# One core, a decoder block and a block of retrieved experts: activations taken two at a time and begun earlier, gathered rows placed anew, first products of a norm in another order

## The chip, the cores and the metric

One Trainium2 chip, one of its cores. The metric is the device time of one execution in microseconds (us), median of three.

## What is computed

Two transformer blocks in a row on x of 256 tokens by 2048 columns, all in float32. `rmsnorm` stands four times ahead of large products: before the first block's projections, before its feed-forward product, before the second block's projections, and before the retrieved experts.

```python
x = x + rmsnorm(mix_out, post_mix_gain)
h = rmsnorm(x, pre_ffn_gain)
f = conv_geglu_ffn(h, w_up, conv_w, conv_b, w_down)
x = x + rmsnorm(f, post_ffn_gain)
...
h = h + concat([a_out, b_out]) @ w_out
h = h + peer(rms_norm(h, g))
return rms_norm(h, final_norm_g)
```

`peer` takes for each token 128 of 16384 experts (rows of 2048 numbers in u and v) with a weight g each:

```python
act = gelu(einsum('td,tkd->tk', xt, u[ids])) * g
out = einsum('tk,tkd->td', act, v[ids])
```

## The kernel before

**Pieces.** All weights stream through SBUF in tiles of 1 MB (`fetch`, three buffers `raw`), each four pieces of 128x512. A float32 piece is split into two fp32r parts: ScalarE (ACT) copies it to `hiR` (`split_hi`, L278), VectorE (DVE) subtracts that from the piece into `loR` (`split_lo`, L286), two pieces per operation, each written out four pieces ahead of use (`LA = 4`), in rings of eight pieces (`NQ`). TensorE (PE) multiplies high by high, high by low and low by high. A piece's end raises the semaphore `piece`; `fetch` waits until the tile three before is wholly split.

**Orders.** There is no scheduler: each engine's program is written out, and steps are placed by the number of the piece beside which they stand.

**The experts.** The first 214 tokens (`TD`) go through dense products with all 16384 experts. They are cut into 128 blocks of 128 experts in three ranges (43, 43 and 42 blocks, `RANGES`). Each range has a **u stage** (four pieces per block, `wide`, L314 and L317; results into `S_`, gelu in place) and a **v stage** (`experts_out`, L1452 and L1455), also four pieces per block, in four passes over the output columns; a piece of its first pass needs its block's activation. In a u stage stand beside the products also the gates: 27 groups per range, three DVE operations each (`dve_gates`, L1329, L1335, L1340), products on PE, and a copy into `G_`. In every range the products with the gates are spread over the u stage by `GATE0` and `GATE_STEP`. The activation of a block is made by three operations on 128x214: DVE multiplies `S_` by `G_` (`dve_gated`, L1418), ACT rounds it to `ah` (`act_act`, L1426), DVE makes the low part `al` (`dve_act`, L1434). They begin twelve pieces before the v stage, one block per piece.

**The rows.** For the last 42 tokens (`TS`) the experts are gathered: 86 operations gather 126 half rows of u and 86 of v (`pool_rows`, L1494, indirect DMA, three buffers `ring`). DVE takes a dot product with each of u (L1515) and adds each of v to `vsum` (L1522). `PLACES` lists the pieces beside which they stand: 31 in the u stages, ten pieces apart, 142 in the v stages, 3.0 to 3.4 apart (one of the 173 places is that of the gelu between u and v).

**The norms.** Ahead of a norm's first product stands a chain: sums, a root, scaling of a quarter of the columns (L360) on DVE; transposes on PE (L371, `pe_norm_turn`); the high part (`act_norm_hi`, L377, semaphore `nhi`) on ACT; the low part (`dve_norm_lo`, L383, `nlo`) on DVE. While it runs, PE computes products that nobody reads (`pe_keep`, L398), `KEEP[i]` of them before and after the first transposes. Then come the first pieces, each quarter of the operand behind a wait for its `nlo`.

**Lambda.** The constants of a recurrence in the second block are made by two ACT operations (L1792, L1794) and 24 small DVE ones (`dve_lambda`), beside the first weights (pieces 0 to 63).

**The end.** The last gain (`gf`), a selection matrix and the residual `xr` are loaded by three DMAs when the third v stage begins (`end_const`); the first to need them stands 72 pieces later.

Of the kernel before, what the change touches and what calls it, by code (L numbers as in the profile page):

```python
# [13 lines left out]
T = 256  # L14
# [31 lines left out]
P_V = 0  # L46
# [43 lines left out]
NROW = 2 * ROWS  # L90
PLACES = [P_U[r] + 4 + 10 * k for r in (1, 2) for k in range((16, 15)[r - 1])]
PLACES += [P_VV[r] + (12, 3, 3)[r] + int((3.0, 3.2, 3.4)[r] * k) for r in range(3) for k in range((52, 51, 39)[r])]
SLOT = {p - P_U[0]: k for k, p in enumerate(sorted(PLACES))}
# [11 lines left out]

ATT = 16 * 8

# [9 lines left out]
def build(nc, A, out):  # L117
# [187 lines left out]
    def wide(e, g, q, X, dst, nt, order=BY_TWO):  # L305
# [13 lines left out]
        m.then_inc(S("piece"), 1)  # L319

    def stationary(e, g, q, X, dst):

        wait_piece(e, g)
        hi, lo = hiR[:, g % NQ, :], loR[:, g % NQ, :]
        for j in range(4):
            k = 4 * q + j
            wh, wl = hi[:, j * 128:(j + 1) * 128], lo[:, j * 128:(j + 1) * 128]
            e.matmul(dst, wh, X.h[:, k, :], start=(k == 0), stop=False)  # L328
            e.matmul(dst, wh, X.l[:, k, :], start=False, stop=False)  # L329
            m = e.matmul(dst, wl, X.h[:, k, :], start=False, stop=(k == KC - 1))  # L330
        m.then_inc(S("piece"), 1)

# [58 lines left out]

    KEEP = [(36, 10), (30, 6), (30, 6), (16, 6)]

# [34 lines left out]
    out_gain = [g1, g3]  # L428
    out_load = [("att_const", ATT), ("ffn_const", 32)]
    out_junk = [junk1, junk2]  # L430
# [875 lines left out]
    GATE0 = [DEC0 + 2 * DECP + 2 - 4 * 16, 1, 1]  # L1306
    GATE_STEP = [3.3, 5.6, 5.4]
    NG = -(-TD // TG)
# [88 lines left out]
    def act_gelu(e, r, s):  # L1397
# [5 lines left out]
        e.activation(S_[:, i, :], S_[:, i, :], ACT.Gelu_apprx_tanh).then_inc(S("s_gelu"), 1)  # L1403

    def dve_gated(e, r, p):
        i0, i1 = RANGES[r]
        i = p + 12
        if 0 <= i < i1 - i0 - 1:
            todo = [i]
        elif i == i1 - i0 + 1:  # L1410
            todo = [i1 - i0 - 1]
        else:
            return
        for i in todo:
            e.wait_ge(S("s_gelu"), i0 + i + 1)
            if i == 0:
                e.wait_ge(S("g_ev"), NG * (r + 1))
            e.tensor_tensor(G_[:, i, :], S_[:, i, :], G_[:, i, :], ALU.mult).then_inc(S("gated_s"), 1)  # L1418

    def act_act(e, r, p):  # L1420
        i = p + 9
        i0, i1 = RANGES[r]
        if not 0 <= i < i1 - i0:
            return
        e.wait_ge(S("gated_s"), i0 + i + 1)
        e.copy(ah[:, i, :], G_[:, i, :]).then_inc(S("a_hi"), 1)  # L1426

    def dve_act(e, r, p):
        i = p + 7
        i0, i1 = RANGES[r]  # L1430
        if not 0 <= i < i1 - i0:
            return
        e.wait_ge(S("a_hi"), i0 + i + 1)
        e.tensor_tensor(al[:, i, :], G_[:, i, :], ah[:, i, :].bitcast(F32), ALU.subtract).then_inc(S("a_lo"), 1)  # L1434

# [137 lines left out]
    def pool_gain(e, f):  # L1573

        cs = quarter(f)
        e.wait_ge(S("end_const"), 48)
# [14 lines left out]
    def pe_rows_sum(e):  # L1591

        e.wait_ge(S("sp_use"), 2 * NROW)
        e.wait_ge(S("end_const"), 48)
        e.wait_ge(S("v_sum"), 16 + 6)
        for f in range(4):
            m = e.matmul(bank[v_bank(2, 2) + f][:, :], sel4[0:GP, :], vsum[0:GP, quarter(f)], start=True, stop=True)
        m.then_inc(S("sp_sum"), 1)

    def dve_rows_sum(e):  # L1600
        e.wait_ge(S("sp_sum"), 1)
        e.wait_ge(S("end_const"), 48)
        e.wait_ge(S("xacc"), 4)
        for f in range(4):
            e.tensor_tensor(xr[:, 1, quarter(f)], xr[:, 1, quarter(f)], bank[v_bank(2, 2) + f][:, :],
                            ALU.add).then_inc(S("sp_x"), 1)

    def dve_y_sum(e, f):
        cs = quarter(f)
        for tb, n in ((0, 128), (1, TD - 128)):  # L1610
            e.wait_ge(S("y_tr"), 2 * f + tb + 1)
            if f == 0:
                e.wait_ge(S("end_const"), 48)
# [16 lines left out]
    def pe_program(e):  # L1630
        e.wait_ge(S("cst"), 3)
        pe_norm_first(e, 0, 0)
        for fb in range(4):
            pair = (2 * (fb % 2), 2 * (fb % 2) + 1)
            if fb >= 2:
                e.wait_ge(S("vt"), 2 * (fb - 1))
            for k in range(KC):
                if fb == 0:
                    pe_norm_next(e, 0, k)
                if fb == 0 and k % 4 == 0:  # L1640
                    e.wait_ge(S("nlo"), 2 * (k // 4) + 2)
                moving(e, P_V + 16 * fb + k, XA.h[:, k, :], XA.l[:, k, :], [bank[b][:, :] for b in pair], k == 0,
                       k == KC - 1)
# [49 lines left out]
        for fb in range(2):  # L1693
            for k in range(KC):
                if fb == 0:
                    pe_norm_next(e, 2, k)
                if fb == 0 and k % 4 == 0:
                    e.wait_ge(S("nlo"), 16 + 2 * (k // 4) + 2)
                moving(e, P_GV + 16 * fb + k, XB.h[:, k, :], XB.l[:, k, :],
                       [bank[2 * fb][:, :], bank[2 * fb + 1][:, :]], k == 0, k == KC - 1)  # L1700
# [36 lines left out]
        for r, (i0, i1) in enumerate(RANGES):  # L1737
# [15 lines left out]
            for f in range(4):  # L1753
# [9 lines left out]
                for i in range(n):  # L1763
                    if f == 0:
                        e.wait_ge(S("a_lo"), i0 + i + 1)
                    experts_out(e, r, f, i)
                    for y in range(3):
                        if r == 2 and n * f + i == Y_AT[y]:
                            pe_y_turn(e, y)
                    if r == 2 and n * f + i == ROWS_AT:  # L1770
                        pe_rows_sum(e)
        pe_end_turn(e)

    def act_program(e):
# [15 lines left out]
        act_norm_hi(e, 0, 3)  # L1790
        e.wait_ge(S("start_const"), 48)
        e.activation(lz[:, 16:32], lv[:, 72:88], ACT.Abs).then_inc(S("lam_a"), 1)  # L1792
        e.wait_ge(S("lam_a"), 1)
        e.activation(lz[:, 0:16], lz[:, 16:32], ACT.Exp, scale=-1.0).then_inc(S("lam_a"), 1)  # L1794
        for i in range(64):
# [4 lines left out]
        for s in range(128):  # L1800
            split_hi(e, P_QK + s + LA)
            if s == 0:
                act_values(e, 3)
            act_attention(e, s)
        for n in range(64):
# [114 lines left out]
    def dve_program(e):  # L1920
# [21 lines left out]
        for i in range(64):  # L1942
            if i + LA >= 10:
                split_lo(e, P_V + i + LA)
            dve_lambda(e, i)
        for s in range(128):
            split_lo(e, P_QK + s + LA)
            dve_attention(e, s)
        for n in range(64):
            if n:  # L1950
                split_lo(e, P_WO + n + LA)
            dve_attention(e, 128 + n)
            if n == 0:
                split_lo(e, P_WO + LA)
# [90 lines left out]
        dve_root(e, 6, st[:, 128:134])  # L2045
        e.wait_ge(S("end_const"), 48)
        e.wait_ge(S("y_out"), 3)
# [68 lines left out]
    def sp_program(e):  # L2116
# [9 lines left out]
        for n in range(NR, NT):  # L2126
            fetch(e, n)
            if n == NR:
# [3 lines left out]
                load(e, "att_const", g1[:, :], A["g_post_mix"].partition_broadcast(128))  # L2132
            elif n == P_WO // 4 + 7:
# [37 lines left out]
            elif n == P_VV[2] // 4 + 4:  # L2171
                e.wait_ge(S("piece"), P_VV[2])
                load(e, "end_const", gf[:, :], A["g_final"].partition_broadcast(128))
                load(e, "end_const", sel4[:, :], A["sel4"])
                load(e, "end_const", xr[:, :, :], xd.ap().rearrange("t p d -> p t d"))
            for p in range(3):
# [133 lines left out]
```

## Time and profile before

| | |
|---|---|
| median of 3 runs | 2891.64 us (2890.97 to 2892.91) |
| the profiled execution | 2892.64 us |
| its span in the trace | 2891.2 us |
| PE busy | 2856.7 us, 99% of the span |
| DVE, ACT, GpSimd busy | 2071.5, 1559.1, 511.2 us |
| granted TensorE clock | 0.999 |
| DMA, mean | 226 GB/s |

Busy time of PE counts the products that nobody reads too. What bounds the kernel is read from what stands between PE's products and from what PE does in the norms' chains.

### The profile page before, as it was taken

To read this page: it belongs to the slowest core of one execution; us is meant where nothing else is said; L and a number is where in the kernel's file an instruction comes from. 1 tells how busy PE (TensorE), PEld (TensorE's weight loads), DVE (VectorE), ACT (ScalarE), POOL (GpSimd) and SP (SyncE) were. 2 spreads that over 40 slices of the span, in tenths; PEclk is the share of its full clock that TensorE was granted. 3 is DMA by queue.
4 is the path that set the end of the run, shared out by engine and by line. 5 is a ranking of instruction groups with operands and counts; after the bars stand their busy time and mean duration, and the time that the engine had idled before them with its cause. 6 is when DMAs were issued, how large, how long until landed. Compare 5 with 4: busy or idle time off the path is not lost.

```text
span 2891.2 us, 45317 instructions
## 1 busy us (share of the span) xinstructions
PE 2856.7 (99%) x18442; PEld 2625.8 (91%) x18442; DVE 2071.5 (72%) x3151; ACT 1559.1 (54%) x2319; POOL 511.2 (18%) x348
## 2 busy tenths in 40 slices
PE   9999999999999999999999999999999999999998
PEld 8888888888888888899899999999999999999997
DVE  5565567666666445666589878888778987778986
ACT  4467755555555444477444656444556444556444
POOL 0011101111111000034111000443011343101631
PEclk9999999999999999999999999999999999999999
DMA  7544455555556555555655656898767898777994
GB/s 265 177 159 141 151 190 184 189 189 188 189 188 221 197 189 175 197 175 170 232 190 175 242 191 211 324 356 331 240 229 247 314 356 313 239 242 255 343 342 152
DMA packets 105658, 654.52 MB, mean 226 GB/s; under 512 B 12526, under 2 KB 13806, under 8 KB 37870
## 3 DMA queue, kind: packets, MB, share of 16 engines
q1 hardware_dynamic: 80684, 561.44, 55.2%
q0 software_dynamic: 24768, 90.19, 8.6%
q8 instruction: 147, 2.41, 0.3%
q14 instruction: 59, 0.48, 0.0%
HBM read 646.29 MB, written 4.19 MB: 225 GB/s over the span
## 4 chain that ended last, share of the span: by engine, by line
PE 82%; DVE 9%; DMA 4%; ACT 3%; issue 2%; SPq 0%; ACTq 0%; DVEq 0%
PE ps L314 26%; PE ps L317 13%; PE ps L1452 8%; PE ps L339 6%; PE ps L341 6%; PE ps L340 6%; PE ps L1455 4%; DMA ring<-in_u_rows_dram,idx 4%; DVE loR L286 4%; PE ps L329 3%; PE ps L328 3%; PE ps L330 3%; DVE ring L1515 2%; DVE hl L1434 1%; ACT hiR L278 1%
## 5 line engine op out<-in xcount | busy, mean ns | idle before, releaser
L286 DVE TENSOR_TENSOR loR<-raw,hiR 128x1024 fp32r<-128x1024 f32 x1017 | 1258.8, 1243 | 695.9 <-ACT hiR L278 692.7
L278 ACT CAST hiR<-raw 128x1024 fp32r<-128x1024 f32 x1026 | 1069.9, 1050 | 789.8 <-PE ps L317 255.3
L314 PE MATMUL ps<-XA,hiR 128*128 128x428 f32 (+1 forms) x3936 | 1240.4, 385 | 2.0 <-DVE loR L286 1.1
L317 PE MATMUL ps<-XA,loR 128*128 128x214 f32 (+1 forms) x3936 | 913.0, 271 | 0.0
L317 PEld LDWEIGHTS ps<-XA,loR 128*128 128x128 f32 x3936 | 748.0, 190 | 83.0
L314 PEld LDWEIGHTS ps<-XA,hiR 128*128 128x128 f32 x3936 | 674.0, 188 | 17.2 <-issue 1.1
L1452 PE MATMUL ps<-hl,hiR 128*128 128x428 f32 x2048 | 582.9, 365 | 9.0 <-DVE loR L286 8.8
L1455 PEld LDWEIGHTS ps<-hl,loR 128*128 128x128 f32 x2048 | 385.3, 188 | 16.3
L1455 PE MATMUL ps<-hl,loR 128*128 128x214 f32 x2048 | 383.6, 269 | 0.0
L1452 PEld LDWEIGHTS ps<-hl,hiR 128*128 128x128 f32 x2048 | 310.5, 192 | 13.2 <-issue 10.9
L1494 POOL DMA_INDIRECT ring<-in_u_rows_dram,idx x86 | 134.7, 1567 | 610.7 <-DVE ring L1515 543.5
L1494 POOL DMA_INDIRECT ring<-in_v_rows_dram,idx x86 | 165.6, 1925 | 362.2 <-DVE vsum L1522 342.4
L340 PE MATMUL ps<-loR,Y 128*128 128x512 f32 x344 | 133.9, 389 | 0.0
L339 PE MATMUL ps<-hiR,Y 128*128 128x512 f32 x344 | 133.9, 389 | 0.0
L341 PE MATMUL ps<-hiR,Y 128*128 128x512 f32 x344 | 133.9, 389 | 0.0
L1515 DVE SCALAR_TENSOR_TENSOR ring<-ring,hrep 126x1024 f32<-126x1024 f32 x86 | 104.8, 1219 | 33.0 <-DMA ring<-in_u_rows_dram,idx 32.9
L862 POOL TENSOR_TENSOR acc<-acc,acc 128x256 f32<-128x256 f32 x43 | 31.9, 741 | 468.9 <-DVE acc L816 468.9
L1522 DVE SCALAR_TENSOR_TENSOR vsum<-ring,gated,vsum 126x1024 f32<-126x1024 f32 x84 | 107.4, 1279 | 6.8 <-DMA ring<-in_v_rows_dram,idx 6.7
L328 PE MATMUL ps<-XB,hiR 128*128 128x256 f32 x384 | 110.1, 287 | 0.0
L329 PE MATMUL ps<-XB,hiR 128*128 128x256 f32 x384 | 108.8, 283 | 0.0
L330 PE MATMUL ps<-XB,loR 128*128 128x256 f32 x384 | 108.7, 283 | 0.0
L1366 ACT ACTIVATE G__145<-ps 128x344 f32<-128x344 f32 (+3 forms) x81 | 37.6, 464 | 127.5 <-PE ps L1356 127.5
(309 smaller groups left out, 3399.0 us busy)
## 6 DMA issues: line engine op xcount, KB each, us to landing
raw<-in_u_dram SPq DMA_DIRECT2D x128, 1024.0 KB, 5.0
raw<-in_v_dram SPq DMA_DIRECT2D x128, 1024.0 KB, 7.4
raw<-in_w_up_dram SPq DMA_DIRECT2D x86, 1024.0 KB, 4.8
raw<-in_w_down_dram SPq DMA_DIRECT2D x43, 1024.0 KB, 4.8
raw<-in_w_in_qk_dram SPq DMA_DIRECT2D x32, 1024.0 KB, 4.9
raw<-in_w_out_dram SPq DMA_DIRECT2D x32, 1024.0 KB, 5.0
raw<-in_w_in_dram SPq DMA_DIRECT2D x24, 1024.0 KB, 4.9
raw<-in_w_in_v_dram SPq DMA_DIRECT2D x16, 1024.0 KB, 4.9
```

What stands on the lines that cost most here:

```text
L278: e.copy(hiR[:, r:r + 2, :], raw[n % NR][:, q:q + 2, :]).then_inc(S("hi"), 1)
L286: e.tensor_tensor(loR[:, r:r + 2, :], raw[n % NR][:, q:q + 2, :], hiR[:, r:r + 2, :].bitcast(F32), ALU.subtract).then_inc(S("lo_pool" if p ...
L314: m = e.matmul(both, hi[:, j * 128:(j + 1) * 128], X.hl[:, :, k, 0:nt], start=(first and n == 0), stop=(last and n == 7), skip_group_check ...
L317: m = e.matmul(dst[:, 0:nt], lo[:, j * 128:(j + 1) * 128], X.h[:, k, 0:nt], start=False, stop=(last and n == 7), skip_group_check=True)
L328: e.matmul(dst, wh, X.h[:, k, :], start=(k == 0), stop=False)
L329: e.matmul(dst, wh, X.l[:, k, :], start=False, stop=False)
L339: e.matmul(dsts[tb], ah_, hi, start=first, stop=False)
L340: e.matmul(dsts[tb], ah_, lo, start=False, stop=False)
L341: m = e.matmul(dsts[tb], al_, hi, start=False, stop=last)
L1452: m = e.matmul(b[:, 0:2 * TD].rearrange("p (a t) -> p a t", a=2), hi[:, j * 128:(j + 1) * 128], hl[:, :, i, :], start=(i == 0), stop=False ...
L1455: m = e.matmul(b[:, 0:TD], lo[:, j * 128:(j + 1) * 128], hl[:, 0, i, :], start=False, stop=(i == i1 - i0 - 1), skip_group_check=True)
L1494: e.indirect_dma_start(ring[m % RN][:, :], None, A["u_rows" if m < NROW else "v_rows"], bass.IndirectOffsetOnAxis(ap=idx[:, m % NROW // 2, ...
```

## The change

- **Activations in pairs.** `dve_gated`, `act_act` and `dve_act` take two blocks each (128x428). In the first range they stand as before, two pieces per pair, from 13 before the v stage. In the second and third a pair stands every 3.8 pieces, from 48 before it; `act_act` three pieces later, `dve_act` five. `GATE_STEP` of these two ranges falls from 5.6 and 5.4 to 4.4, so that all gates are done by then.
- **Rows.** 52 places in the u stages: 20 from piece 4, 5.5 apart, and 6 from piece 120, 8 apart, in each. First v stage: 42 from piece 30, 3.3 apart. The other two: 6 from piece 3, 6 apart, then 40 and 27 from piece 40, 3.2 and 3.45 apart.
- **First products of a norm.** In the first and third, products with the high operand need only `nhi`, then come the ones with `loR`, then those with the low operand. In the second, the `loR` products of two pieces come first; in the fourth, the 16 products of two pieces that need only the high operand. `KEEP` is cut.
- **Lambda** moves: ACT's part to piece 20 of the query and key products, DVE's beside the first output projection.
- **Loads.** `end_const` in twelve parts, one behind each of twelve fetches; the attention's constants six tiles later, `g1` at tile 20.

```diff
-PLACES = [P_U[r] + 4 + 10 * k for r in (1, 2) for k in range((16, 15)[r - 1])]
...
+PLACES = [P_U[r] + 4 + int(5.5 * k) for r in (1, 2) for k in range(20)]
+PLACES += [P_U[r] + 120 + 8 * k for r in (1, 2) for k in range(6)]
...
-    KEEP = [(36, 10), (30, 6), (30, 6), (16, 6)]
+    KEEP = [(36, 6), (28, 3), (28, 3), (10, 3)]
...
-    GATE_STEP = [3.3, 5.6, 5.4]
+    GATE_STEP = [3.3, 4.4, 4.4]
...
+    def moving_first(e, g, i, q, first, xh, xl, dsts):
+
+        hi, lo = hiR[:, g % NQ, :], loR[:, g % NQ, :]
+        e.wait_ge(S("hi"), g // 2 + 1)
+        for tb in range(2):
+            e.wait_ge(S("nhi"), 8 * i + 2 * q + tb + 1)
+            e.matmul(dsts[tb], xh[:, half(tb)], hi, start=first, stop=False)
+        wait_piece(e, g)
+        for tb in range(2):
+            e.matmul(dsts[tb], xh[:, half(tb)], lo, start=False, stop=False)
+        for tb in range(2):
+            e.wait_ge(S("nlo"), 8 * i + 2 * q + tb + 1)
+            m = e.matmul(dsts[tb], xl[:, half(tb)], hi, start=False, stop=False)
...
+    def pair_at(r, p):
+
+        return [k for k in range(NPAIR[r]) if (2 * k - 13 if r == 0 else int(3.8 * k) - 48) == p]
...
             if j == 0:
+                e.wait_ge(S("nhi"), 8 + 2 * q + 2)
+                for c in range(2):
+                    wide_part(e, P_UP + n + c, q, XA, bank[c], T, "low")
                 e.wait_ge(S("nlo"), 8 + 2 * q + 2)
-            wide(e, P_UP + n, q, XA, bank[j], T)
+            if j < 2:
+                wide_part(e, P_UP + n, q, XA, bank[j], T, "high")
+            else:
+                wide(e, P_UP + n, q, XA, bank[j], T)
...
             if c == 0:
+                e.wait_ge(S("nhi"), 24 + 2 * q + 2)
+                for b in range(QQ):
+                    stationary_part(e, P_Q + n + b, q, XA, bank[b][:, 0:T], "high")
                 e.wait_ge(S("nlo"), 24 + 2 * q + 2)
-            stationary(e, P_Q + n, q, XA, bank[c][:, 0:T])
+            stationary_part(e, P_Q + n, q, XA, bank[c][:, 0:T], "low")
```

PE at the third norm, ahead of the products with `XB`; `x30` and `x6` are the unread products. Before:

```order
L398 MATMUL ps<-ident 128x128 x30
L371 MATMUL ps<-ident,tmp_113 128x128 x8
L398 MATMUL ps<-ident 128x128 x6
L339 MATMUL ps<-hiR,XB 128x512
L340 MATMUL ps<-loR,XB 128x512
L341 MATMUL ps<-hiR,XB 128x512
```

Now:

```order
L446 MATMUL ps<-ident 128x128 x28
L419 MATMUL ps<-ident,tmp_113 128x128 x8
L446 MATMUL ps<-ident 128x128 x3
L372 MATMUL ps<-hiR,XB 128x512 x2
L375 MATMUL ps<-loR,XB 128x512 x2
L378 MATMUL ps<-hiR,XB 128x512 x2
```

Five unread products are gone, and the two that read the low operand (L378) stand last.

DVE in the second range's v stage, between the subtractions for its pieces 18 and 22. Before:

```order
L286 TENSOR_TENSOR loR<-raw_50,hiR 128x1024
L1418 TENSOR_TENSOR G__145<-S__144,G__145 128x214
L1434 TENSOR_TENSOR hl<-G__145,hl 128x214
L1418 TENSOR_TENSOR G__145<-S__144,G__145 128x214
L1434 TENSOR_TENSOR hl<-G__145,hl 128x214
L1515 SCALAR_TENSOR_TENSOR ring_164,dots<-ring_164,hrep 126x1024
L286 TENSOR_TENSOR loR<-raw_51,hiR 128x1024
L1418 TENSOR_TENSOR G__145<-S__144,G__145 128x214
L1434 TENSOR_TENSOR hl<-G__145,hl 128x214
L1418 TENSOR_TENSOR G__145<-S__144,G__145 128x214
L1434 TENSOR_TENSOR hl<-G__145,hl 128x214
L286 TENSOR_TENSOR loR<-raw_51,hiR 128x1024
```

Now:

```order
L289 TENSOR_TENSOR loR<-raw_50,hiR 128x1024
L1482 TENSOR_TENSOR hl<-G__145,hl 128x428
L1563 SCALAR_TENSOR_TENSOR ring_165,dots<-ring_165,hrep 126x1024
L289 TENSOR_TENSOR loR<-raw_51,hiR 128x1024
L1470 TENSOR_TENSOR G__145<-S__144,G__145 128x428
L1482 TENSOR_TENSOR hl<-G__145,hl 128x428
L289 TENSOR_TENSOR loR<-raw_51,hiR 128x1024
```

Where eight short operations stood, three of twice the length do; the rest stands in the u stage ahead.

## Rows read from the trace of the kernel before

**Rows 1.** Waits of PE: by line, who released it; us in total, times, longest.
```profile
PE ps L1452 <- DVE loR L286: 8.8, 19, 0.8
```
**Rows 2.** Timeline, first norm: start, duration, engine, operation, count, [idle before <- releaser].
```profile
14.86 2.35 DVE L286 TENSOR_TENSOR loR<-raw,hiR 128x1024 fp32r<-128x1024 f32 x2
16.44 0.47 PE L339 MATMUL ps<-hiR,XA 128*128 128x512 f32 x1
...
29.59 1.29 DVE L383 TENSOR_TENSOR XA<-ps,XA 128x512 fp32r<-128x512 f32 x2 [2.60 <-ACT XA L377]
29.93 0.23 ACT L1792 ACTIVATE lz<-lv 128x16 f32<-128x16 f32 x1
30.18 1.28 ACT L1794 ACT_TABLE_LOAD   x1
...
31.60 3.87 ACT L278 CAST hiR<-raw 128x1024 fp32r<-128x1024 f32 x4
...
33.94 0.50 PE L339 MATMUL ps<-hiR,XA 128*128 128x512 f32 x1 [1.83 <-DVE loR L286]
```
**Rows 3.** Timeline, third norm, PE and DVE.
```profile
1151.97 1.42 DVE L360 SCALAR_TENSOR_TENSOR tmp<-x,st,g 128x512 f32<-128x512 f32 x2
1153.24 1.04 PE L371 MATMUL ps<-ident,tmp 128*128 128x128 f32 x8
...
1154.49 1.29 DVE L383 TENSOR_TENSOR XB<-ps,XB 128x512 fp32r<-128x512 f32 x2 [0.45 <-ACT XB L377]
...
1155.84 0.50 PE L339 MATMUL ps<-hiR,XB 128*128 128x512 f32 x1 [0.22 <-DVE XB L383]
```
**Rows 4.** Timeline, fourth norm, PE.
```profile
1451.69 2.65 PE L371 MATMUL ps<-ident,tmp 128*128 128x128 f32 x16
1454.17 1.50 PE L398 MATMUL ps<-ident 128*128 128x128 f32 x12
1455.43 0.36 PE L328 MATMUL ps<-XA,hiR 128*128 128x256 f32 x1
```
**Rows 5.** Stretches: us, busy PE, PEld, DVE, ACT, POOL, clock, DMA share, GB/s.
```profile
30.00:36.00 6.00, 4.17 (x19) 3.14 (x18) 4.19 (x7) 5.44 (x8) 0.00 (x0) 1.00 0.15 35
1787.00:1822.00 35.00, 35.00 (x229) 34.08 (x229) 35.00 (x73) 21.55 (x41) 6.76 (x5) 1.00 0.74 254
2047.00:2110.00 63.00, 63.00 (x527) 60.80 (x526) 47.85 (x72) 34.49 (x57) 6.63 (x5) 1.00 0.72 244
```
**Rows 6.** Timeline of DVE: a late row of the first v stage, then the third.
```profile
1992.23 1.23 DVE L1515 SCALAR_TENSOR_TENSOR ring<-ring,hrep 126x1024 f32<-126x1024 f32 x1 [2.83 <-DMA ring<-in_u_rows_dram,idx]
...
2689.49 1.22 DVE L286 TENSOR_TENSOR loR<-raw,hiR 128x1024 fp32r<-128x1024 f32 x1
2690.62 0.37 DVE L1418 TENSOR_TENSOR G__145<-S__144,G__145 128x214 f32<-128x214 f32 x1
2690.91 0.38 DVE L1434 TENSOR_TENSOR hl<-G__145,hl 128x214 fp32r<-128x214 f32 x1
2691.21 1.28 DVE L1522 SCALAR_TENSOR_TENSOR vsum<-ring,gated,vsum 126x1024 f32<-126x1024 f32 x1
2692.40 0.37 DVE L1418 TENSOR_TENSOR G__145<-S__144,G__145 128x214 f32<-128x214 f32 x1
```
**Rows 7.** One line in a stretch: first v stage (L1452, L1515), second u stage (L314).
```profile
L1452 PE MATMUL ps<-hl,hiR x688: 352/365/468, 1783.1 to 1998.7; 128*128 128x428 f32 x172
...
L314 PE MATMUL ps<-XA,hiR x688: 361/371/460, 1999.1 to 2223.2; 128*128 128x428 f32 x172
...
  DMA ring<-in_u_rows_dram,idx: 28.4, 24
```
**Rows 8.** Timeline of DVE, second u stage: a gate's first operation, and what follows its last.
```profile
2001.48 0.33 DVE L1329 TENSOR_TENSOR OI<-sel_ij,ioh 128x352 f16<-128x352 f16 x1
...
2002.77 2.35 DVE L286 TENSOR_TENSOR loR<-raw,hiR 128x1024 fp32r<-128x1024 f32 x2
```
**Rows 9.** DMA issues in the third v stage: KB, us to landing.
```profile
xr<-x_mid SPq DMA_DIRECT2D x1, 2048.0 KB, 12.3
```

More of the change, by code:

```diff
@@ L102, in quarter @@
     return slice(fb * 512, (fb + 1) * 512)
-ATT = 16 * 8
+ATT = 16 * 7
 class Mat:
@@ L319, in wide, with wide_part, stationary_part @@
         m.then_inc(S("piece"), 1)
+    def wide_part(e, g, q, X, dst, nt, part):
+        wait_piece(e, g)
+        both = dst[:, 0:2 * nt].rearrange("p (a t) -> p a t", a=2)
+        for j in range(4):
+            k, cs = 4 * q + j, slice(j * 128, (j + 1) * 128)
+            if part == "low":
+                m = e.matmul(dst[:, 0:nt], loR[:, g % NQ, cs], X.h[:, k, 0:nt], start=(k == 0), stop=False,
+                             skip_group_check=True)
+            else:
+                m = e.matmul(both, hiR[:, g % NQ, cs], X.hl[:, :, k, 0:nt], start=False, stop=(k == KC - 1),
+                             skip_group_check=True)
+        if part == "high":
+            m.then_inc(S("piece"), 1)
+    def stationary_part(e, g, q, X, dst, part):
+        wait_piece(e, g)
+        hi, lo = hiR[:, g % NQ, :], loR[:, g % NQ, :]
+        for j in range(4):
+            k = 4 * q + j
+            wh, wl = hi[:, j * 128:(j + 1) * 128], lo[:, j * 128:(j + 1) * 128]
+            if part == "high":
+                e.matmul(dst, wh, X.h[:, k, :], start=(k == 0), stop=False)
+                m = e.matmul(dst, wl, X.h[:, k, :], start=False, stop=False)
+            else:
+                m = e.matmul(dst, wh, X.l[:, k, :], start=False, stop=(k == KC - 1))
+        if part == "low":
+            m.then_inc(S("piece"), 1)
     def stationary(e, g, q, X, dst):
@@ L1640, in pe_program @@
                 if fb == 0 and k % 4 == 0:
-                    e.wait_ge(S("nlo"), 2 * (k // 4) + 2)
+                    moving_first(e, P_V + k, 0, k // 4, k == 0, XA.h[:, k, :], XA.l[:, k, :],
+                                 [bank[b][:, :] for b in pair])
+                    continue
                 moving(e, P_V + 16 * fb + k, XA.h[:, k, :], XA.l[:, k, :], [bank[b][:, :] for b in pair], k == 0,
@@ L1790, in act_program @@
         act_norm_hi(e, 0, 3)
[L1791 to L1794, printed above, removed]
         for i in range(64):
@@ L1803, in act_program @@
                 act_values(e, 3)
+            if s == 20:
+                e.wait_ge(S("start_const"), 48)
+                e.activation(lz[:, 16:32], lv[:, 72:88], ACT.Abs).then_inc(S("lam_a"), 1)
+                e.wait_ge(S("lam_a"), 1)
+                e.activation(lz[:, 0:16], lz[:, 16:32], ACT.Exp, scale=-1.0).then_inc(S("lam_a"), 1)
             act_attention(e, s)
@@ L2127, in sp_program @@
             fetch(e, n)
-            if n == NR:
+            if n == P_QK // 4 + 4:
+                load(e, "att_const", g1[:, :], A["g_post_mix"].partition_broadcast(128))
+            elif n == NR + 6:
                 for dst, name in ((cosT, "cosT"), (sinT, "sinT"), (am_dl, "am_dl"),
@@ L2172, in sp_program @@
                 e.wait_ge(S("piece"), P_VV[2])
-                load(e, "end_const", gf[:, :], A["g_final"].partition_broadcast(128))
                 load(e, "end_const", sel4[:, :], A["sel4"])
-                load(e, "end_const", xr[:, :, :], xd.ap().rearrange("t p d -> p t d"))
+            if P_VV[2] // 4 + 4 <= n < P_VV[2] // 4 + 8:
+                cs = quarter(n - P_VV[2] // 4 - 4)
+                load(e, "end_const", gf[:, cs], A["g_final"][cs].partition_broadcast(128))
+            if P_VV[2] // 4 + 8 <= n < P_VV[2] // 4 + 16:
+                tb, q = divmod(n - P_VV[2] // 4 - 8, 4)
+                load(e, "end_const", xr[:, tb, quarter(q)], xd[tb][:, quarter(q)])
             for p in range(3):
```

70 lines of the change are left out of this document (35 added, 35 removed).

## The prediction

> **What bounds the kernel now.** I read the waits of TensorE (PE) first, since it is busy 99% of the span: only what it waits for, and the products that nobody reads, can be won. The largest entry is the v products waiting for `loR`, 8.8 us in 19 waits [rows 1]. The timeline adds one wait of 1.83 us behind the first norm [rows 2]. Then I read the chains of the norms, where unread products hide a wait [rows 3, 4], and last DVE's load beside the products, by the stretches and the distances of its operations from start to start [rows 5, 6].
>
> **Why the v products wait.** DVE is busy 35.00 of 35 us early in the first v stage, and 47.85 of 63 in a u stage [rows 5]. From start to start a subtraction for two pieces takes 1.13 us, one activation operation 0.29, a row 1.19 [rows 6], 1.23 with the dot product's readout. PE gives each piece 215.6/172 = 1.25 us in a v stage and 224.1/172 = 1.30 in a u stage [rows 7]. While activations run, a piece of the second v stage asks of DVE 0.57 + 2 x 0.29 + 1.23/3.2 = 1.53 us. Over 30 pieces that is 8 us of arrears, against a lead of four pieces, 5 us: the rest, about 3 us in each v stage, is the 8.8 us of PE's waits. So they are arrears of one engine, and work moved to where it has room removes them.
>
> **Part 1, pairs and places.** An operation on 128x428 isn't in the trace. Below it stands the 128x214 one, 0.29 us; above it the 512-element one: two take 1.29 us with one's own duration of 0.69 [rows 3], so 0.60 apart. On the line between them 428 is 0.51; two separate ones, 0.58, are the upper bound. I take 0.51. DVE's load per piece is then:
> - second and third v stage, to piece 31: 0.57 + 2 x 0.51/3.8 + 1.23/6 = 1.04 of 1.25;
> - first v stage to piece 30, without rows: 0.57 + 0.51 = 1.08; after it 0.57 + 1.23/3.3 = 0.94;
> - u stages to piece 120: a gate's three operations take 2002.77 - 2001.48 = 1.29 us [rows 8], so 0.57 + 0.07 (one sum per block) + 1.29/4.4 + 1.23/5.5 = 1.15 of 1.30. It was 1.29/5.6 + 1.23/10 + 0.64 = 0.99.
> - last 48 pieces of a u stage: 0.57 + 0.07 + 0.27 + 1.23/8 = 1.06.
>
> Nowhere is it above what PE gives. Bunching remains: a sum of the v stage before (about 2 us), a gate and a subtraction meet at the start of a u stage, but they did before and PE did not wait. With the upper bound of 0.58 the largest v load is 1.15, still below 1.25. I forecast 8.4 of the 8.8 us gone; bounds 4 and 8.8. ACT's third of the pairs adds nothing, as it is half idle (21.55 of 35 [rows 5]).
>
> **Part 2, lambda.** At 29.93 ACT makes two small operations with a table load of 1.28 us between; the next split starts at 31.60 [rows 2]. DVE has finished its low part at 30.88. Without lambda the split starts at 29.93, 1.67 earlier, and the subtraction is bound by it. The wait of 1.83 shrinks to about 0.3: **1.5 us**, bounds 0 and 1.83. The table load is not lost: attention's first exponential must now load it, behind an idle ACT, and the 24 small DVE operations stand where DVE waits for pieces. I cost both at nothing; if the cover is gone it is one load, 1.3 us, once.
>
> **Part 3, the norms.** Unread products are 12 in 1.50 us, each `KEEP` being two, so one `KEEP` is 0.24 us [rows 4]. The first norm: four fewer let PE start at 15.5 instead of 16.44; two high products run, then `loR` is there (14.86 + 1.22 = 16.1 [rows 2]). The piece ends near 17.1 instead of 17.9: **0.7 us**, bounds 0 and 0.95. The third: the scaled quarter's first half is ready at 1152.7, the transposes begin at 1153.24 only because unread products stand before them; they can begin 0.35 earlier. Then 0.72 us of unread products replace 1.5, and the first product needs the high part, not DVE's low part that ended at 1155.78. PE starts near 1154.75 instead of 1155.84 [rows 3]: **1.1 us**. The second norm has the same chain: **1.1**. Bounds of each 0.3 and 1.4. The fourth: the unread products end at 1454.17 + 0.72 = 1454.9, and the first product starts then instead of 1455.43 [rows 4]: **0.5**, bounds 0 and 0.7. The six dropped before its transposes win nothing: those wait for the scaling and PE stands idle for 1.4 us in their place. Behind each norm the next quarters' transposes, high parts and splits are released by PE's own transposes, so they move with it; `nlo` of the next quarter is due more than 1 us after it is ready.
>
> A word on the clock. PE's granted clock is 1.00, its level of 2.4 GHz, in 30 to 36 us, around an idle time of 1.83 us [rows 5, 2]; the new idle time of 1.4 us is shorter, so I put no cost on it. The Trainium skill (TensorE: Matmul & The Clock Gate, HAM oscillation) warns of idle gaps that take the clock to half rate. [...]
>
> **Part 4, loads.** The same bytes, in twelve parts. In the burst now the 2 MB part lands after 12.3 us [rows 9]; first use is 72 pieces, 90 us, behind the stage's start. Cost nothing, bounds -0.5 and +1. The attention's constants leave the first 22 us and stand beside a tile with three tiles' lead: nothing. The Trainium skill (DMA: Bandwidth & Descriptors, Bandwidth) wants DMAs of at least 1 MiB for 75% of peak. These become 256 KB each, and by that rule they hold up the tiles they are mixed with.
>
> **Sum.** 8.4 + 1.5 + 0.7 + 1.1 + 1.1 + 0.5 = 13.3 us. The profiled execution took 2892.6, so 2879.3; the median of the runs is 1.0 lower, so **2878.3 us**. The bounds together: about 4.6 to 16.5 us of gain.
>
> **Rivals.**
> 1. *Tiles and rows, not DVE's arrears, hold part of the v products.* For it: 24 of the first v stage's rows kept DVE waiting, 28.4 us in all [rows 7], and rows remain dense behind piece 40, where the third stage's twelve parts meet them. Against: in the second v stage, with rows 3.2 apart, PE never waited once the arrears were worked off. Then half of Part 1 stays: gain 9, 2882.6 us. Chance 0.10. The 1 MiB rule would act through this mechanism; it is in this chance.
> 2. *The norms' chains do not follow.* PE comes earlier but DVE's backlog of scaling, new x and low parts does not move, and the 1 us returns as a wait for the second quarter. Gain 8.4 + 1.5 + 0.7 = 10.6: 2881 us. Chance 0.08.
> 3. *The v waits are not touched*, because they only move to another place (bunches of pairs and dense rows from piece 40). Gain 4.9: 2886.7. Chance 0.06, all of it within 0.2%.
> 4. *Slower: a late row in the u stage.* DVE takes its operations in order, so a row that has not landed stops subtractions and gates. At 5.5 pieces apart the room is 5.5 x 0.15 = 0.8 us per row. The waits of the first v stage average 28.4/24 = 1.2 us [rows 7], the longest is 2.83 [rows 6]. Were the mean between them, 2.0, 40 rows would cost 40 x 1.2 = 48 us, less the 13.3 gained: 2926. It decides for slower by more than a measurement tells from a mean of 0.8 + (13.3 + 5.8)/40 = 1.3 us. For it: that is nearly the mean of those waits. Against: the transport is busy 0.72 in a u stage [rows 5], and none of the 16 rows there made DVE wait. Chance 0.03.
> 5. *Slower or level: the clock falls in the fourth norm.* The stretch to the next transposes, about 3 us, would take twice that. It gives back 3 us: 2881. Chance 0.03; it changes the time, not the sign.
>
> **How the numbers follow.** The forecast has 0.70. A measurement of this kernel can tell about 0.2%, 5.8 us, from no change. Forecast, cases 1, 2 and 5 are faster by more: 0.91, less 0.03 for two of them together and for what I have not seen. Within 0.2%: case 3 and most of those, 0.08. Slower: case 4 and the rest, 0.04. The range: from 15.6 us of gain, near the sum of the upper bounds, to 7 us, which takes in cases 1, 2 and 5: 2876 to 2884.6. It leaves out case 3, case 4 and the combinations, 0.12, and the forecast's own tails.
>
> **What the profile would show.** Part 1: the v products' waits for `loR` below 1 us in all, DVE with idle time in the first 40 us of each v stage, 128x428 operations of 0.59 us (0.51 apart), u stages that keep 1.30 us a piece. Part 2: no table load near 30 us, a PE wait of 0.3 us there. Part 3: first products 1.0 to 1.2 us nearer to the scaling in the second and third norm, no new wait at the second quarter, clock 1.00 throughout. Part 4: twelve issues of 256 KB, none followed by a late tile. The prediction is wrong if DVE still has no idle time in the v stages, or if u products wait for gates.

## Result, and the profile of the changed kernel

| | before | changed |
|---|---|---|
| median of four runs, us | 2892.22 (2890.97 to 2892.91) | 2872.97 (2872.68 to 2873.28) |
| ratio, 95% interval | | 0.9931 (0.9916 to 0.9946) |
| span in the trace | 2891.2 | 2871.9 |
| DVE, GpSimd busy | 2071.5, 511.2 | 2070.2, 502.9 |

The gain is 19.3 us. The forecast was 13.3 (2878.3 us), its range ended at 2876.0: the sign and the places were right, the size was too small.

Waits of PE in the changed kernel (line, released by; us in total, times, longest). The v products' line, L1452 before and L1500 now, is absent: the 8.8 us of [rows 1] are gone. L659, in the attention, had the same 6.5 us before.

```profile
PE ps L659 <- DVE tsb L812: 6.5, 6, 1.1
PE ps L419 <- DVE tmp L408: 1.4, 1, 1.4
PE ps L387 <- DVE loR L289: 1.4, 3, 0.9
PE ps L1616 <- DVE yT L1608: 1.2, 4, 0.5
```

Stretches of the changed kernel, columns as in [rows 5]: behind the first norm, the fourth norm, early first v stage, second u stage.

```profile
30.00:36.00 6.00, 5.83 (x26) 4.51 (x25) 5.07 (x6) 4.22 (x5) 0.00 (x0) 1.00 0.58 197
1446.00:1452.00 6.00, 4.57 (x35) 3.86 (x36) 5.60 (x11) 2.64 (x5) 0.00 (x0) 1.00 0.00 0
1781.00:1816.00 35.00, 35.00 (x230) 34.09 (x229) 32.26 (x45) 21.78 (x30) 0.00 (x0) 1.00 0.63 211
2041.00:2104.00 63.00, 63.00 (x553) 60.63 (x553) 53.53 (x83) 35.38 (x59) 13.07 (x9) 1.00 0.76 261
```

DVE has room in the v stage (32.26 of 35 us, 35.00 before) and pays for it in the u stage (53.53 of 63, 47.85 before). That is 85% of PE's 1.30 us a piece, 1.10; I had worked out 1.15.

**Where the 19.3 us are.** I take a stage's start as the start of its first product, and count the third v stage to the start of its last one. Up to the first u product (1556.17 before, 1551.23 now) the change wins 4.94 us. Then, in us:

| | u1 | v1 | u2 | v2 | u3 | v3 |
|---|---|---|---|---|---|---|
| before | 226.94 | 216.03 | 224.42 | 217.60 | 219.54 | 217.15 |
| changed | 226.95 | 211.73 | 224.30 | 211.73 | 219.39 | 212.72 |

The v stages win 4.30 + 5.87 + 4.43 = 14.60, the u stages 0.26; the tail behind the last product gives back 0.5. 4.94 + 14.60 + 0.26 - 0.5 = 19.3. The forecast for these v stages was 8.4, and 4.9 for all ahead of them. So one term, the v stages, carries the error.

**Why 8.8 us of reported waits were worth 14.6.** PE's timeline of the kernel before, one of the reported waits:

```profile
2261.66 0.57 PE L1452 MATMUL ps<-hl,hiR 128*128 128x428 f32 x2
2262.07 0.37 PE L1455 MATMUL ps<-hl,loR 128*128 128x214 f32 x2
2262.28 0.57 PE L1452 MATMUL ps<-hl,hiR 128*128 128x428 f32 x2
2262.69 0.37 PE L1455 MATMUL ps<-hl,loR 128*128 128x214 f32 x2
2263.80 0.63 PE L1452 MATMUL ps<-hl,hiR 128*128 128x428 f32 x2 [0.74 <-DVE loR L286]
```

Behind a group of L1455 the next one of L1452 starts 0.21 us later (2262.07 to 2262.28). Here it is 2263.80 - 2262.69 = 1.11, so 0.90 us are lost and 0.74 reported. The idle time counts from the end of the last product, and products overlap: their ends reach 0.16 us into what would have been the next one's time. Each wait hides as much, and the shortest of the 19 on the list has 0.16 us of idle time: what is shorter is not listed at all. From one group of L1452 to the next it takes 0.615 us undisturbed. Those that took over 0.04 us more cost 4.28 us in the first v stage and 5.84 in the second (18 in each), of which the list has 2.13 in 5 waits and 3.79 in 9. An undisturbed v stage is then 216.03 - 4.28 = 211.75, and 211.73 is what it now takes. That is 211.73/172 = 1.23 us a piece; the 1.25 that I took for what PE gives [rows 7] had the waits in it.

The first norm, PE in the changed kernel: the wait of 1.83 us [rows 2] is 0.17.

```profile
31.07 0.39 PE L389 MATMUL ps<-hiR,XA 128*128 128x512 f32 x1
31.63 0.50 PE L387 MATMUL ps<-hiR,XA 128*128 128x512 f32 x1 [0.17 <-DVE loR L289]
```

The third norm, PE: the transposes start 0.45 us nearer to the chain's start at 1143.13 than before, and the first product 7.99 us behind it (9.30 before).

```profile
1143.13 6.41 PE L446 MATMUL ps<-ident 128*128 128x128 f32 x56
1149.38 1.31 PE L419 MATMUL ps<-ident,tmp 128*128 128x128 f32 x8
1150.53 0.83 PE L446 MATMUL ps<-ident 128*128 128x128 f32 x6
1151.12 0.75 PE L372 MATMUL ps<-hiR,XB 128*128 128x512 f32 x2
```

The fourth norm, PE: the idle time foreseen stands there, the granted clock stays at 1.00 (second stretch above).

```profile
1443.59 2.39 PE L446 MATMUL ps<-ident 128*128 128x128 f32 x20
1447.41 2.64 PE L419 MATMUL ps<-ident,tmp 128*128 128x128 f32 x16 [1.43 <-DVE tmp L408]
1449.89 0.83 PE L446 MATMUL ps<-ident 128*128 128x128 f32 x6
1450.48 0.36 PE L347 MATMUL ps<-XA,hiR 128*128 128x256 f32 x1
```

### The profile page after: what moved, and what is told of

The parts are those of the page before. It is cut to its first block, busy times and chain, and to the rows that moved or that the text cites. A ratio compares the mean times of both kernels' runs of the same rounds, so it can differ in the third digit from the quotient of the medians.

```text
span 2871.9 us, 45054 instructions
## 1 busy us (share of the span) xinstructions
PE 2846.4 (99%) x18396; PEld 2617.6 (91%) x18396; DVE 2070.2 (72%) x3025; ACT 1555.1 (54%) x2256; POOL 502.9 (18%) x348
## 4 chain that ended last, share of the span: by engine, by line
PE 92%; ACT 3%; DVE 2%; issue 2%; DMA 1%; POOL 0%; SPq 0%; ACTq 0%; DVEq 0%; POOLq 0%
PE ps L317 27%; PE ps L1500 14%; PE ps L320 13%; PE ps L1503 8%; PE ps L387 5%; PE ps L388 5%; PE ps L389 5%; PE ps L362 3%; PE ps L361 3%; PE ps L363 3%; PE ps L1404 1%; ACT hiR L281 1%; PE ps L446 1%; DVE loR L289 1%; PE ps L419 1%
## 5 line engine op out<-in xcount | busy, mean ns | idle before, releaser
L1500 PE MATMUL ps<-hl,hiR 128*128 128x428 f32 x2048 | 580.9, 364 | 0.0
L1500 PEld LDWEIGHTS ps<-hl,hiR 128*128 128x128 f32 x2048 | 310.3, 191 | 0.5 <-issue 0.5
L1542 POOL DMA_INDIRECT ring<-in_u_rows_dram,idx x86 | 142.8, 1660 | 614.1 <-DVE ring L1563 546.9
L1542 POOL DMA_INDIRECT ring<-in_v_rows_dram,idx x86 | 148.4, 1725 | 348.2 <-DVE vsum L1570 331.4
```

The costliest lines, as they stand in the source:

```text
L1500: m = e.matmul(b[:, 0:2 * TD].rearrange("p (a t) -> p a t", a=2), hi[:, j * 128:(j + 1) * 128], hl[:, :, i, :], start=(i == 0), stop=False ...
L1542: e.indirect_dma_start(ring[m % RN][:, :], None, A["u_rows" if m < NROW else "v_rows"], bass.IndirectOffsetOnAxis(ap=idx[:, m % NROW // 2, ...
```

## Experiments

My theory after the result: the gain in the v stages is all arrears of DVE, 13 to 14.6 us from start to start, and any way of freeing DVE there wins it. Rivals: rows or tiles that came late held part of it; the wider operations rather than the places bring it; the front has a share in it. All runs but the last are one execution each. The kernel before, on the same chip, took 2893.09 us beside the front, the rows and both pair runs; 2892.19 beside the rows with parts, the short rows, lambda back and the first run of the better version; 2891.21 to 2904.94 in seven executions (median 2896.66) beside the loads in three, the single blocks, DVE filled up and the timed run; 2901.71 beside the last two on gathers. So the later runs are read against the other runs and not against it. I compare v stages by their lengths.

**The front alone.** The norms, `KEEP`, lambda and the attention's constants as changed; activations, rows, gates and end's loads as before.

```diff
-    KEEP = [(36, 10), (30, 6), (30, 6), (16, 6)]
+    KEEP = [(36, 6), (28, 3), (28, 3), (10, 3)]
...
+                    moving_first(e, P_V + k, 0, k // 4, k == 0, XA.h[:, k, :], XA.l[:, k, :],
```

> The kernel before with the change's norms, unread products, lambda and constants alone; places, gates, activations and the end's loads as before. Both theories: the span falls by 4.9 us (the first u product of the experts started 4.9 us earlier in the changed kernel), to about 2886.3, and the v products still wait as before, 8.8 us reported in 19 waits. If the norms only gave back time that the v stages then needed, the fall is under 3.

2886.44 us. The first u product starts at 1550.82, 5.35 earlier than before; the v stages take 214.88, 217.20 and 217.83 us, 0.9 less in all, and PE's list has the old entry:

```profile
PE ps L1497 <- DVE loR L286: 9.0, 18, 0.8
```

Front and v stages are separate terms, but for that 0.9. Of the 5.35 us the changed kernel has 4.94: it lost 0.4 to a late weight tile ahead of the fourth norm that this run did not meet (told with the norms below).

**The rows' places alone.** Only `PLACES` as in the change.

> The kernel before with the new places of the rows alone; activations one block per operation, twelve pieces ahead. Theory of arrears: DVE's load while activations run is 0.57 + 0.58 + 1.23/6 = 1.36 us per piece of 1.25 in the second and third v stage, 4 us of arrears over 36 pieces against a lead of 5, so nearly all of the 14 us goes: span down by 12 to 14. If the earlier start of the activations is what counts, down by less than 7. If late tiles and rows are what counts, down by 2 to 4, since the dense part is almost as dense as before.

2882.70. The v stages take 211.73, 211.73 and 217.18: the first two are clean with single activations at their old places. The third kept its loss, 4.46 us: one late row of 6.2 us for DVE, waits of 0.36 and 1.71 us for PE, 2.4 us of them from start to start, and behind the longer one, from 2710.08 on, the granted clock at the level of 1.2 GHz for 3.4 us:

```profile
2710.00:2713.50 3.50, 3.50 (x13) 3.35 (x13) 3.46 (x4) 0.00 (x0) 0.81 (x2) 0.51 0.76 255
```

PE computes there at half rate, so my estimate of what the fall cost is half of 3.4, 1.7 us. Part of the expectation failed in this stage, and the rows of GpSimd, which issues the gathers, show why (start, duration):

```profile
2657.21 7.45 POOL L1497 DMA_INDIRECT ring<-in_v_rows_dram,idx  x1 [11.89 <-DVE vsum L1525]
2665.32 7.45 POOL L1497 DMA_INDIRECT ring<-in_v_rows_dram,idx  x1 [0.65 <-DVE vsum L1525]
2673.42 7.45 POOL L1497 DMA_INDIRECT ring<-in_v_rows_dram,idx  x1 [0.65 <-DVE vsum L1525]
2681.53 20.42 POOL L1497 DMA_INDIRECT ring<-in_v_rows_dram,idx  x1 [0.65 <-DVE vsum L1525]
```

and DVE at the end of the last one:

```profile
2698.79 2.35 DVE L289 TENSOR_TENSOR loR<-raw,hiR 128x1024 fp32r<-128x1024 f32 x2
2707.34 1.28 DVE L1525 SCALAR_TENSOR_TENSOR vsum<-ring,gated,vsum 126x1024 f32<-126x1024 f32 x1 [6.20 <-DMA ring<-in_v_rows_dram,idx]
```

In this gather DVE had no pause until it ran into the row itself at 2701.14; the gather ended 0.81 us later, at 2701.95. In the changed kernel the gathers of the third v stage take 1.7 to 1.9 us:

```profile
2650.33 1.68 POOL L1542 DMA_INDIRECT ring<-in_v_rows_dram,idx  x1 [10.43 <-DVE vsum L1570]
2657.26 1.68 POOL L1542 DMA_INDIRECT ring<-in_v_rows_dram,idx  x1 [5.25 <-DVE vsum L1570]
```

The kernel before had it too, unnoticed: in this stage eleven gathers took 2.8 to 5.2 us.

```profile
2666.64 4.56 POOL L1494 DMA_INDIRECT ring<-in_v_rows_dram,idx  x1 [33.19 <-DVE vsum L1522]
2671.86 3.43 POOL L1494 DMA_INDIRECT ring<-in_v_rows_dram,idx  x1 [0.66 <-DVE vsum L1522]
```

Each of the eleven ended 0.89 or 0.90 us after DVE began the sum of a row, and so did the three of 7.45 us above: dense rows end a gather early. It is no rule, as the gather of 20.42 us passed two such sums (2688.09 and 2695.03).

So a DVE that never pauses can hold up the very gather that it will wait for. The Trainium skill (SBUF — State Buffer, SBUF: two separate sides) tells of this: GpSimd writes the descriptors of its DMAs through a port that it shares with VectorE, and some VectorE operations keep it out. These rows fit that picture, but they do not show the port.

**Rows' places, and the end's loads in twelve parts.** The 3 MB burst of those loads fell beside the late row, so it had to be told apart.

> The kernel before with the new places of the rows and the end's loads in twelve parts. Leading theory (DVE leaves GpSimd no room): in the third v stage of the rows-only run DVE was busy 49.93 of 50 us and each gather took GpSimd 6.07 us instead of 1.9, so rows came late whatever the loads do; then the third v stage is again 4 to 5 us longer than 212.7, its gathers take over 4 us each, time near 2882.5. Rival (the 3 MB burst of the end's loads delayed those rows): with the loads in twelve parts the third v stage falls to 212.7 to 213.5, the gathers take 2 us, time near 2878.5.

2886.64. v stages 211.73, 211.73, 219.23; gathers of 7.45 us four times and one of 14.64; a PE wait of 4.1 us, and the clock's fall behind it again (0.51 in 2717.00 to 2720.50). Without the burst it was no better (2.1 us worse in that stage, most of it the longer wait): the burst is not needed for the late row.

**Pairs, late.** Pairs of blocks at `2 * k - 13` in all three ranges; rows, gates and the rest as before.

> The kernel before with activations in pairs in their old places (from 13 pieces ahead, one block per piece in all ranges), old rows and gates. Theory of arrears: load 0.57 + 0.51 + 0.38 = 1.46 per piece of 1.25 in place of 1.53, so arrears of 7.5 us in place of 10 over 36 pieces, the waits fall by about half: span down by 5 to 8. If tiles are what counts: down by less than 2.

2884.58. v stages 212.83, 213.86, 214.35: 9.7 us won, more than expected. Waits of v products on the list: 2.8 us in 5.

**Pairs, early.** As the change places them, with its `GATE_STEP`; rows as before.

> The kernel before with pairs from 48 pieces ahead and the denser gates, rows in their old places. Theory of arrears: second and third v stage 0.57 + 0.27 + 0.38 = 1.22 of 1.25, no wait left there (10 us); the first still 0.57 + 0.51 + 0.41 = 1.49 from piece 12 to 36, 6 us of arrears, 1 to 2 us of its 4.1 left: span down by 11 to 13, u stages unchanged. If rows as dense as before at the start of a v stage are what counts: down by less than 6.

2881.30. v stages 212.83, 211.73, 212.92, 13.3 won; u stages as before. One wait of 0.7 us is left, in the first range, where pairs stand late. Early pairs alone win nearly all, rows alone all of it in the first two stages (10.1 us) and nothing in the third: the two parts overlap.

**Short rows.** The kernel before, each row operation of DVE on 64 of its 1024 columns, so the last tokens' experts are left out for the other columns. All gathers stay.

```diff
+                rg, cs = rg[:, 0:64], slice(cs.start, cs.start + 64)
```

> The kernel before with all gathers as they were, but the row operations of DVE (dot product, sum into vsum) work on 64 of 1024 columns, so the experts of the last tokens are left out for most columns. DVE loses about 0.95 us per row, the transfers stay. Arrears theory: in a v stage a piece then asks 0.57 + 0.58 + 0.28/3.2 = 1.24 us of DVE while activations run, which is what PE gives; the waits of the v products fall to below 1.5 us, v stages to 212 to 213, gain 11 to 14 us, time 2879 to 2882. Rival (the rows' transfers or the weights' tiles hold the v products): the waits stay at 6 us or more, time above 2887.

2879.53, a fall of the clock ahead of the second norm included (see the run with lambda back). No wait of a v product; stages 211.73, 211.73, 212.77, 14.55 us won. The transfers are all there (654.52 MB in either profile), only DVE's work is less: the whole 14.6 was DVE's arrears, and rival 1 of the prediction falls. Gathers of up to 4.6 us in the third stage remain, and no v product waits.

**Single blocks at the pairs' places.** The changed kernel with DVE's operations on 128x214 again.

```diff
+            for i in range(two.start, two.stop):
+                m = e.tensor_tensor(G_[:, i, :], S_[:, i, :], G_[:, i, :], ALU.mult)
+            m.then_inc(S("gated_s"), 1)
...
+            for i in range(two.start, two.stop):
+                m = e.tensor_tensor(al[:, i, :], G_[:, i, :], ah[:, i, :].bitcast(F32), ALU.subtract)
+            m.then_inc(S("a_lo"), 1)
```

> The changed kernel with DVE's activation operations of one block each again (two where there was one of 128x428), at the pairs' early places. Theory (it is the early, spread places that bring the gain): DVE is asked for 0.58 instead of 0.51 per two blocks, 1.15 of 1.25 us per piece at most, v stages stay at 211.7 and 212.7, time 2873 within 0.5 us. Rival (the wider operations bring it): v stages 1 us or more longer, 2876 or above.

2873.13; stages 211.73, 211.73, 212.72. The width is worth nothing here, the places are.

**The end's loads in three.** The changed kernel with `end_const` as before.

> The changed kernel with the end's constants in three loads as before, all else as changed. Theory: with DVE and the tiles in slack, the burst of 3 MB stops nothing, third v stage 212.7, time within 0.5 us of the changed kernel's 2873. Rival: the burst delays a gathered row or a tile, one stall of 1 to 5 us in the third v stage, 2874 to 2878.

2873.03, inside the changed kernel's own 2872.68 to 2873.28. The 2 MB part lands after 12.4 us again and no v product waits. Twelve parts are worth nothing.

**Lambda back.** The changed kernel with lambda beside the first weights.

> The changed kernel with the constants of the recurrence (lambda) back beside the first weights, all else as changed. Theory: ACT's table load and two small operations stand ahead of the fourth split again, PE waits for it some 1.8 us near 31 us and gets nothing back: time 2874.5 to 2875, first u product 1.5 to 2.0 later than in the changed kernel. Rival (the first norm's earlier start alone brought that gain; the split would not be late any more): no wait over 0.5 us near 31 us and time 2873.

2875.83, more than expected. The chain of the second norm begins 3.17 us later than in the changed kernel (421.38 against 418.21), 1.5 us more than the waits explain (1.80 against 0.17). PE and its stretches say where that is:

```profile
33.17 0.54 PE L387 MATMUL ps<-hiR,XA 128*128 128x512 f32 x1 [1.80 <-DVE loR L289]
33.51 0.63 PE L388 MATMUL ps<-loR,XA 128*128 128x512 f32 x1
33.93 0.63 PE L389 MATMUL ps<-hiR,XA 128*128 128x512 f32 x1
```

```profile
33.20:36.00 2.80, 2.80 (x7) 2.27 (x8) 2.73 (x7) 1.50 (x2) 0.00 (x0) 0.55 0.70 187
36.00:42.00 6.00, 6.00 (x26) 4.86 (x25) 3.18 (x7) 2.10 (x2) 0.00 (x0) 0.92 0.81 291
```

Behind the idle time the products start 0.42 us apart instead of 0.23: the granted clock fell to the level of 1.2 GHz for some 3.4 us. The first u product is only 2.63 us later: 0.5 us came back between the third norm and the fourth, where that weight tile came in time in this run. In the kernel before, an idle time of 1.83 us in the same place left it at 1.00 [rows 5]. The other profiles that have this wait decide it both ways: at 1.00 in the rows-only run, fallen in both pair runs, in the short-row run, in the rows-and-loads run and in the first of the accumulator runs below. In these five the second norm's chain begins 1.5 to 1.8 us later than in the profile of before (422.08 to 422.32 against 420.54), though nothing ahead of it was changed. In none of the eight profiles with lambda moved is there such a wait, or a fall in this place. The Trainium skill (TensorE: Matmul & The Clock Gate, HAM oscillation) warns of idle gaps that take the clock to half rate. The gaps that it speaks of are longer than this one; here a gap of 1.8 us did so in six profiles of eight, and the measurement decides.

**DVE filled up.** As the run with single blocks, and in the third range each operation in four column parts. This adds only the fixed cost of instructions.

```diff
+                for c in range(0, 214, 54 if r == 2 else 214):
+                    cs = slice(c, min(c + (54 if r == 2 else 214), 214))
+                    m = e.tensor_tensor(G_[:, i, cs], S_[:, i, cs], G_[:, i, cs], ALU.mult)
```

> As the run with single blocks, and in the third range each DVE activation operation is cut in four column parts of 54 numbers, the same results. Each part costs a fixed 0.06 us more, so a pair asks 0.9 us more of DVE, 0.25 us per piece: 1.3 where PE gives 1.25, for the last 48 pieces of the third u stage and 31 of the v stage. Theory (DVE without a pause keeps GpSimd from issuing gathers): DVE is busy 49 or more of 50 us there, each gather takes GpSimd over 3 us instead of 1.7, and PE waits little, since the arrears stay below the lead, unless a row comes late. Rival (the gathers' length comes from the DMA traffic or the dense rows of the other placing): the gathers stay at 1.7 to 2 us.

2881.91, 9 us more. The third u stage takes 221.93 (its products wait 1.7 us for `S_`), the v stage 219.24. One gather took GpSimd 23 us, over two rows and 20 us of other DVE work, and the row behind it stopped DVE and then PE (3.9 us, and the granted clock is at 0.50 in 2684.00 to 2688.00):

```profile
2653.90 23.11 POOL L1550 DMA_INDIRECT ring<-in_v_rows_dram,idx  x1 [11.05 <-DVE vsum L1578]
```

```profile
2680.90 1.29 DVE L1578 SCALAR_TENSOR_TENSOR vsum<-ring,gated,vsum 126x1024 f32<-126x1024 f32 x1 [4.69 <-DMA ring<-in_v_rows_dram,idx]
```

The gather ended at 2677.01, 0.80 us after DVE went idle at 2676.21. PE waited more than I had expected, since the late row does come.

**What lets a gather through.** In the second v stage of the rows-only run, gathers of u rows took 1.68 us beside an equally full DVE (50.00 of 50 us). The u rows' dot product is followed by a read of the accumulator, the v rows' sum is not. Two runs add it (its result is not read), to the rows-only run and to the filled-up run.

```diff
-                e.scalar_tensor_tensor(vsum[0:GP, cs], rg, gated[0:GP, j:j + 1], vsum[0:GP, cs], ALU.mult, ALU.add).then_inc(
-                    S("sp_use"), 1)
+                e.scalar_tensor_tensor(vsum[0:GP, cs], rg, gated[0:GP, j:j + 1], vsum[0:GP, cs], ALU.mult, ALU.add,
+                                       accum_out=dots[0:GP, j, m % 2:m % 2 + 1]).then_inc(S("sp_use"), 1)
```

> The run with the rows' new places alone, with each sum of a v row also giving a sum per row that nobody reads, so that a read of the accumulator follows it as it does behind the dot product of a u row. Theory (that read leaves GpSimd its moment): the gathers of v rows in the third v stage fall from 7.45 and 20.4 us to about 1.7, no row comes late, the third v stage is 212.7, time 2878.5 within 1 us. Rival (it is the third stage or the v rows' table, not DVE's stream): gathers stay above 5 us and the time at 2882 or above.

2880.68, with the clock's fall behind the first norm in it (1.4 us later than the rows-only run at the second norm). The third v stage takes 213.41 instead of 217.18, and the gathers are short:

```profile
2658.99 1.68 POOL L1497 DMA_INDIRECT ring<-in_v_rows_dram,idx  x1 [13.03 <-DVE vsum L1525]
2667.10 1.68 POOL L1497 DMA_INDIRECT ring<-in_v_rows_dram,idx  x1 [6.44 <-DVE vsum L1525]
2675.22 1.69 POOL L1497 DMA_INDIRECT ring<-in_v_rows_dram,idx  x1 [6.43 <-DVE vsum L1525]
```

> The run with DVE's activation operations cut in four in the third range, with the same added read behind each sum of a v row. Theory: the gather that took 23.1 us takes about 1.7, the late row and PE's stall of 3.9 us go, only the waits of the u products (2.5 us in that stage) and some arrears stay: time 2876 to 2878. Rival: the long gather and the stall stay, 2881 to 2883.

2882.53. Here it did not help: the gather at 2654.03 took 23.16 us again, although two such reads fell into it, and PE waited 3.5 us, with the clock at 0.50 in 2684.00 to 2688.00 again; the later gathers went down from 6.93 and 2.81 to 1.68 us. So the read behind a row frees a gather in one stream of DVE's operations and not in the other. What exactly GpSimd needs of DVE stays open.

**A better version.** The changed kernel, with one step of PE in the attention, L659, a piece later: it waited for DVE in six heads, 1.08 us each.

```diff
-            elif d == 8:
+            elif d == 9:
                 e.wait_ge(S("sb_sp"), h + 1)
```

> The changed kernel with one step of PE in the attention (the running sums over later keys, which wait for DVE 1.08 us in six heads) beside the next piece, 9 instead of 8. If DVE's and ACT's steps behind it have room (DVE stood idle 3.25 us shortly before), the six waits of 1.08 us, some 1.24 from start to start, go: 7 us, 2866. Rival: the wait only moves to DVE's step behind it, its subtractions come late and PE waits for them: 2873, no gain.

2865.47. The entry of 6.5 us is gone from PE's list, one wait grew from 0.5 to 0.8 us (the query and key copy), and the one behind the late tile is now long enough to be listed, with 0.3. 7.5 us for six waits of 1.08 is 1.25 each: 0.17 above the listed idle time, near the 0.16 of the v stages. Timed:

> The changed kernel with the attention's step one piece later, timed. One look gave 2865.5 and no wait in its place: 2865 to 2866, ratio to the kernel before 0.9905 to 0.991.

2865.32 us median of four (2865.29 to 2866.10), ratio to the kernel before 0.9893 (0.9874 to 0.9912), on a chip where the kernel before took 2896.66 in the median of seven and 2891.21 at best. It beats both kernels, the changed one (2872.97) by 7.65 us.

## The prediction, step by step

- **What bounds the kernel, and why the v products wait: right.** DVE's arrears, nothing else (short rows: 14.55 of 14.60 us). DVE was foreseen to have idle time in the v stages, and has.
- **Part 1: the step that failed.** "About 3 us in each v stage, is the 8.8 us of PE's waits" took the list of waits as the whole loss and made it the upper bound. Measured: 14.6 us, 4.30, 5.87 and 4.43. The list leaves out 0.16 us of each of the 19 waits, 3.0 us, and all that are shorter, the other 2.8. The arrears' own sum was a second warning: I had set 8 us of them against a lead of 5, taken PE's rate as 1.25 and not 1.23, and left out what was behind the 30th piece. An upper bound of 14.6 would have come from PE's starts. The upper bounds as written add up to 15.1 us, 15.6 with the loads, and not to the 16.5 of the sum.
- **Parts' costs: right in what mattered.** 128x428 takes 0.597 us, foreseen 0.59. No u product waits for gates, u stages keep their length. Single blocks (0.58 for two) give the same time, as the load of 1.15 said.
- **Part 2, lambda: 1.5 foreseen.** The wait went from 1.83 to 0.17 us. The run that puts it back is 3.17 us behind at the second norm, 1.6 by the wait and 1.5 by the clock, and 2.63 at the first u product. Costing the moved operations at nothing was right: the rest of PE's list is unchanged up to the second norm.
- **Part 3, norms.** First 0.7: with lambda back the product behind the wait starts at 33.17 instead of 33.94, 0.77. Second 1.1: its chain is 8.40 instead of 9.50 us. Third 1.1: chain 7.99 instead of 9.30, 1.31, but 0.4 of it went again ahead of the fourth norm. A weight tile came late there: ACT waited 5.22 us for it, against 4.04 with the front alone and 4.00 with lambda back. A product of PE that waits for DVE (1399.89) then lost 0.4 us with an idle time of 0.13, too short for the list; those two runs have no such wait. Why the tile was later stays open. Fourth 0.5: chain 6.89 instead of 7.56, 0.67. In all 4.94 with lambda, foreseen 4.9.
- **The clock.** It held at 1.00 over 1.43 us of idle in the fourth norm, in all nine profiles that have it. But my argument, that an idle time of 1.83 us had left it at 1.00, rested on one profile: in six others the same wait was followed by a fall, in one it was not. The waits of 1.7 to 4.1 us in the third v stage of four runs all have a fall with them.
- **Part 4: 0 foreseen, 0.06 us measured** (2872.97 and 2873.03), less than the spread of either kernel.
- **Rivals.** 1 and 3 are refuted by the short rows and by the result. 2 did not come. 4 did not come: no row made DVE wait in a u stage, nine u rows did in the v stages, 8.1 us in all (26 and 32.9 us before), and no u stage grew. Its mechanism is real in another place: in four runs with a full DVE a late row in the third v stage went with 4 to 7 us more. Of that PE's waits are 2.4 to 4.8 us from start to start, and the rest, 1.8 to 3.1 us, goes with the clock's fall. The changed kernel stands clear of it, as far as the runs show, because DVE has room there (busy 40.86 us of that stage's first 50; 50.00 in the rows-only run). 5 did not come.

## To carry to other kernels

Measure what a wait costs from start to start, against the same group undisturbed; the listed idle time is a lower bound, and with many short waits far below. Look at the granted clock behind a wait too: here it cost up to as much as the wait. Engines that work through a fixed order go into arrears where load is dense: spread the work to where they have room, whatever its width. Leave DVE pauses where GpSimd gathers rows for it, and look at the length of GpSimd's gathers when it has none.

## What the runs showed of the hardware

- A gather that takes GpSimd 1.68 us took 2.8 to 5.2, 7.45, 14.6, 20.4 and 23.1 us while DVE never paused, and two of the longest ended 0.80 and 0.81 us after DVE's first pause. Fourteen others ended 0.89 or 0.90 us after DVE began a row's sum. Beside u rows, with a DVE as full, gathers took 1.68.
- The same idle time of 1.8 us of PE in the same place was followed by a fall of the granted clock to the level of 1.2 GHz in six profiles (1.5 to 1.8 us lost) and by none in two. A gap of 1.43 us in another place was followed by none in nine.
- The idle time listed between products of the v stages is 0.16 us less than what PE loses.
